# Stick-breaking attention with its later sums on top of the scores, values of two pairs in split passes, and a new order of the mixed phase

## What is computed

```python
def stick_breaking_attention(h, w_in, w_out):
    q, k, v = jnp.split(h @ w_in, 3, axis=-1)          # 16 heads of 64
    ...
        z = jnp.einsum('bhqd,bhkd->bhqk', qb, k) * scale
        past = k_pos[None, :] < q_pos[:, None]
        log_beta = jax.nn.log_sigmoid(z)
        log_keep = jnp.where(past, jax.nn.log_sigmoid(-z), 0.0)
        later = lax.cumsum(log_keep, axis=3, reverse=True) - log_keep
        a = jnp.where(past, jnp.exp(log_beta + later), 0.0)
        return jnp.einsum('bhqk,bhkd->bhqd', a, v)
    ...
    return merge_heads(o) @ w_out
```

## Time and profile before

| | |
|---|---|
| median of 3 runs | 2287.86 us (2287.84 to 2290.86) |
| profiled execution | 2294.6 us, span 2292.8 us |
| PE busy | 2175.9 us, 95% |
| DVE busy | 1593.8 us, 70% |
| ACT busy | 1094.7 us, 48% |
| mean granted TensorE clock | 0.982 |

### The profile page before, as it was taken

One profiled execution on the slowest core, in us unless ns is written; L12 is line 12 of the kernel. 1 busy time (PEld: TensorE's weight loads), 2 busy tenths in 40 slices (PEclk: granted clock), 3 DMA queues, 4 the chain that ended last, 5 costly groups with the idle time before them and its releaser, 6 DMA issues.

```text
span 2292.8 us, 44979 instructions
## 1 busy us (share of the span) xinstructions
PE 2175.9 (95%) x17598; PEld 2068.1 (90%) x17598; DVE 1593.8 (70%) x2647; ACT 1094.7 (48%) x1755; POOL 0.2 (0%) x4
## 2 busy tenths in 40 slices
PE   7889999998899999998999999999898999998999
PEld 6788899987888999897999887999787999897999
DVE  6585688865857888666787766788777855666544
ACT  4454444445445444555444455444465444555443
POOL 0000000000000000000000000000000000000000
PEclk9999999999999999999999999999999999999999
DMA  5454499845445998443799644799544875442664
GB/s 159 130 142 139 144 299 299 282 127 137 131 129 165 300 304 274 132 134 104 259 301 301 182 130 129 231 302 299 165 113 137 285 202 174 129 137 83 188 187 147
DMA packets 546483, 436.40 MB, mean 190 GB/s; under 512 B 27680, under 2 KB 472264, under 8 KB 546248
## 3 DMA queue, kind: packets, MB, share of 16 engines
q1 hardware_dynamic: 545208, 433.16, 62.1%
q10 hardware_dynamic: 1168, 1.77, 0.2%
HBM read 433.82 MB, written 1.05 MB: 190 GB/s over the span
## 4 chain that ended last, share of the span: by engine, by line
PE 83%; DVE 8%; ACT 4%; DVEq 1%; issue 1%; DMA 1%; SPq 1%; ACTq 0%
PE bank L690 13%; PE bank L692 13%; PE bank L691 13%; PE acc L690 8%; PE acc L692 7%; PE acc L691 7%; PE bank L840 3%; PE bank L898 2%; PE bank L1214 2%; PE bank L700 2%; DVE w_lo L1840 1%; ACT w_hi L1349 1%; PE bank L761 1%; PE bank L762 1%; PE bank L765 1%
## 5 line engine op out<-in xcount | busy, mean ns | idle before, releaser
L1349 ACT ACTIVATE w_hi<-wslot 128x1024 fp32r<-128x1024 f32 x590 | 611.5, 1055 | 532.8 <-PE acc L692 250.6
L690 PE MATMUL bank<-h_hi,w_hi 128*128 128x256 f32 x2784 | 792.6, 285 | 21.7 <-DVE w_lo L1831 7.8
L691 PE MATMUL bank<-h_lo,w_hi 128*128 128x256 f32 x2784 | 778.0, 279 | 0.0
L692 PE MATMUL bank<-h_hi,w_lo 128*128 128x256 f32 x2784 | 777.8, 279 | 0.0
L1840 DVE TENSOR_TENSOR w_lo<-wslot,w_hi 128x1024 fp32r<-128x1024 f32 x412 | 493.7, 1221 | 214.9 <-ACT w_hi L1349 214.2
L690 PEld LDWEIGHTS bank<-h_hi,w_hi 128*128 128x128 f32 x2784 | 526.3, 189 | 39.7 <-DVE w_lo L1831 13.6
L691 PEld LDWEIGHTS bank<-h_lo,w_hi 128*128 128x128 f32 x2784 | 531.0, 191 | 2.3 <-issue 1.7
L692 PEld LDWEIGHTS bank<-h_hi,w_lo 128*128 128x128 f32 x2784 | 526.0, 189 | 0.0
L690 PE MATMUL acc<-mid_hi,w_hi 128*128 128x256 f32 x1120 | 318.0, 284 | 6.3 <-DVE mid_lo L2180 3.2
L692 PE MATMUL acc<-mid_hi,w_lo 128*128 128x256 f32 x1120 | 313.0, 279 | 0.0
L691 PE MATMUL acc<-mid_lo,w_hi 128*128 128x256 f32 x1120 | 313.0, 279 | 0.0
(11 more groups left out here) (288 smaller groups left out, 2970.7 us busy)
## 6 DMA issues: line engine op xcount, KB each, us to landing
wslot<-in_ada_w_dram SPq DMA_DIRECT2D x192, 512.0 KB, 5.8
wslot<-in_ffn_w_gate_dram SPq DMA_DIRECT2D x88, 512.0 KB, 4.9
wslot<-in_ffn_w_up_dram SPq DMA_DIRECT2D x88, 512.0 KB, 5.5
wslot<-in_ffn_w_down_dram SPq DMA_DIRECT2D x88, 512.0 KB, 3.7
wslot<-in_w_in_dram SPq DMA_DIRECT2D x72, 512.0 KB, 5.1
wslot<-in_sb_w_in_dram SPq DMA_DIRECT2D x48, 512.0 KB, 4.9
wslot<-in_w_ffn_gate_dram SPq DMA_DIRECT2D x44, 512.0 KB, 4.7
wslot<-in_w_ffn_up_dram SPq DMA_DIRECT2D x44, 512.0 KB, 5.3
```

Source lines behind the costliest of these rows:

```text
L690: pe.matmul(dst, w_hi[:, w, cols], hi, start=start, stop=False, skip_group_check=True)
L691: pe.matmul(dst, w_hi[:, w, cols], lo, start=False, stop=False, skip_group_check=True)
L692: return pe.matmul(dst, w_lo[:, w, cols], hi, start=False, stop=stop, skip_group_check=True)
L1349: return act.activation(dst, src, ACT.Copy)
```

## The change

It has three parts.

**Stick-breaking.** Scores and later sums are now one accumulation in PSUM: the scores don't end their group, the later sums go on top with masked negative log terms in `lb`, and `end_weights` subtracts `sm` from the bank. The scale of the scores moves into ACT's copy of the query. ACT reads the scores straight from PSUM. The values of two pairs are projected at once in three split passes from slots 2 and 4 (`V_SLOTS`), so each has a `w_hi` and `w_lo` of its own (`PART_V`), and `hT` isn't made for these layers. The order on all engines is new: after the scores of pair j come the output of pair j-1, the query of j+1, the later sums of j, the key of j+1, the values of j, half of the values' projection of the next two pairs, and the scores of j+1.

**Mixed phase.** Some operations trade places on PE, ACT and DVE. **Sliding window.** Unit 2's parts are made inside pair 0.

```diff
 # schedule: norm no longer makes hT for "sb"
-        if split != "ffn" or more["stack"] == 1:
+        if split == "ffn" and more["stack"] == 1 or split == "att" and more["att"] != "sb":
             counts.update(h_ready=KT)
...
 # SP, stick-breaking (need = uses of the slot that must be over)
+                        query_and_key([offs[c] + P for c in range(2)], [u[c] + 2 for c in range(2)])
+                        out_rows(0, u[3] + 1)
                         first_units(2, l, u[SLOT_FF:SLOT_FF + 2])
+                        values([offs[2] + 2 * P + b * P for b in range(2)], [u[V_SLOTS[b]] + 2 for b in range(2)])
+                        query_and_key([offs[c] + 2 * P for c in range(2)], [u[c] + 3 for c in range(2)])
...
 # PE, stick
                 def scores(i, first=False):
                     pe.wait_ge(sem["qk_ready"], g("qk_ready") + i + 1)
+                    if not first:
+                        pe.wait_ge(sem["y_ready"], g("y_ready") + i)
...
-                        pe.matmul(bank[:, 2 + hh, 0:256], C("later"), sm[:, hh, 0:256], start=True, stop=False)
+                        pe.matmul(bank[:, 2 + hh, 0:256], C("later"), lb[:, hh, 0:256], start=False, stop=False, skip_group_check=True)
...
-                        mm = pe.matmul(B(1, 256 + P * t, 384 + P * t), hT[:, k, P * t:P * t + P], wk(2, k),
-                                       start=(k == 0), stop=(k == KT - 1))
+                        high, low = (w[:, PART_V:PART_V + 2, k_cols(k)] for w in (w_hi, w_lo))
+                        pe.matmul(dst, h_hi[:, k, tokens], high, start=(k == 0), stop=False, skip_group_check=True)
+                        pe.matmul(dst, h_hi[:, k, tokens], low, start=False, stop=False, skip_group_check=True)
+                        mm = pe.matmul(dst, h_lo[:, k, tokens], high, start=False, stop=(k == KT - 1), skip_group_check=True)
...
+                def whole(m, b, first=False, more=True, v=True):
+                    j = 2 * m + b
+                    if not first:
+                        out(j - 1)
+                    if more:
+                        query(j + 1)
+                    later_sums(j)
+                    if more:
+                        key(j + 1)
+                    values(m, b)
+                    if v:
+                        project_v(m + 1, b)
+                    if more:
+                        scores(j + 1)
...
 # ACT, stick
+                    softplus(j)
+                    if b == 0:
+                        v_high(m + 1)
+                    act.wait_ge(unit_done[3], g("unit_done3") + j)
+                    out_high(j)
+                    exps(j)
+                    act.wait_ge(unit_done[0], g("unit_done0") + j + 2)
+                    mix_high(0, 0, unit_loads(at, "sb", 0, j + 2))
+                    qk_copy(j + 1)
+                    y_high(j)
+                    mix_high(1, 1, unit_loads(at, "sb", 1, j + 2))
+                    if b == 1:
+                        v_copy(m + 1)
...
 # DVE, stick
+                        dve.wait_ge(sem["sb_log"], g("sb_log") + 2 * i + hh + 1)
+                        stt(sm[:, hh, :], z, 0.0, pr[:, hh, :], ALU.max, ALU.add)
+                        dve.drain()
+                        stt(lb[:, hh, :], sm[:, hh, :], -1.0, C("past")).then_inc(sem["sb_spm"], 1)
...
+                    softplus(j)
+                    if b == 0:
+                        v_low(m + 1)
+                    else:
+                        mix_low(3, PART_DOWN, j)
+                    end_weights(j)
+                    if b == 0:
+                        mix_low(3, PART_DOWN, j)
+                    mix_low(0, 0, j + 2)
+                    out_low(j)
+                    mix_low(1, 1, j + 2)
...
+                softplus(n - 1)
+                mix_low(3, PART_DOWN, n - 1)
+                low(0, 2, g("w_high") + 3)
+                end_weights(n - 1)
+                out_low(n - 1)
...
 # PE, mixed phase: ssd_tokens is cut in two, ssd_products is its second half
+                def ssd_products(gr):
                     after("ssd_cumc", gr + 1)
...
                 out(12, 0, mix_y[0])
+                ssd_products(1)
                 out(13, 1, mix_y[0])
...
                 gla_scores(1)
+                after("gla_yl", 1)
+                out(28, 0, mix_y[0], hi=4)
                 gla_values(1)
-                after("gla_yl", 1)
-                out(28, 0, mix_y[0])
+                out(28, 0, mix_y[0], lo=4)
...
 # ACT, mixed phase
-                gate_exps(0)
...
+                unit_high(11)
                 ssd_square(0)
-                unit_high(11)
                 ssd_root(0)
                 unit_high(12)
                 unit_high(13)
+                ssd_silu(1)
                 y_high("ssd", 0, mix_y[0])
-                ssd_silu(1)
...
+                gate_exps(0)
                 ssd_square(1)
...
 # DVE, mixed phase
                 unit_low(3)
+                unit_low(4)
                 convolve(0, 0)
-                unit_low(4)
-                gate(0)
                 unit_low(5)
...
                 unit_low(9)
+                unit_low(10)
+                unit_low(11)
                 ssd_gated(0)
-                unit_low(10)
                 convolve(1, 0)
-                unit_low(11)
                 convolve(1, 1)
+                ssd_normed(0)
                 unit_low(12)
-                ssd_normed(0)
+                y_low("ssd", 0, mix_y[0])
                 unit_low(13)
-                y_low("ssd", 0, mix_y[0])
...
                 unit_low(16)
+                gate(0)
                 ssd_gated(1)
...
 # ACT and DVE, sliding window (here ACT; DVE with qk_low and next_low alike)
-                if att == "swa":
-                    qk_high(2)
...
-                    if att != "swa":
+                    if att != "swa" or i == 0:
                         next_high(i + 2)
```

More of the change, by code:

```diff
@@ L121 @@
 PART_SECOND = 3
+PART_V = 2
+V_SLOTS = (2, 4)
 def split_index(what, f):
@@ new lines, in stick @@
+                v_high(0)
+                qk_copy(0)
+                for c in range(2):
+                    mix_high(c, c, unit_loads(at, "sb", c, 1))
+                v_copy(0)
+                with act.Fori(0, n // 2 - 1) as m:
+                    whole(m, 0)
+                    whole(m, 1)
+                softplus(n - 2)
+                act.wait_ge(unit_done[3], g("unit_done3") + n - 2)
+                out_high(n - 2)
+                exps(n - 2)
+                act.wait_ge(unit_done[0], g("unit_done0") + n)
@@ L1897, in stick, with v_low @@
[L1897 to L1901 removed]
+                def v_low(m):
+                    for b in range(2):
+                        dve.wait_ge(sem["v_high"], g("v_high") + 2 * m + (b + 1))
+                        part = PART_V + b
+                        dve.tensor_tensor(w_lo[:, part, :], wslot[:, V_SLOTS[b], :], w_hi[:, part, :], ALU.subtract)\
+                           .then_inc(slot_used[V_SLOTS[b]], 1)
```

237 lines of the change are left out of this document (118 added, 119 removed).

## The result

The median fell from 2287.86 us to 2259.68 us (3 runs, 2254.85 to 2259.87). The ratio is 0.9861 (95% interval 0.984 to 0.9881), so 31.8 us are gained, 27 to 37 by the interval. The forecast was 18.6 (2269.3, range 2258 to 2279).

The account below looks back on a forecast made before the run. TensorE (PE), busy 95% of the span, was taken as the bound, so only its work or waits could pay. Stick-breaking -16.8, mixed phase -6.6 and sliding window +4.8 sum to -18.6 us: 2269.3 from 2287.9, range 2258 to 2279.

Parts of the forecast that it names:

- the mixed phase: Two mixed layers: reordering cuts PE's waits by 2.3 and 1.0 us a layer, -6.6 us in all.
- the edges of SB: Start and end of each stick-breaking layer: start waits lose 1.4 us, clock returns 0.8, the end gains 1.5.
- Values in three passes, and the loop: Stick-breaking loop: three split passes save 0.94 us a pair, 7.5 a layer; pairs take 14.80 us without waits.
- the clock at both ends: Stick-breaking layer: lower-clock loss recovered, 0.8 us at the start and 1.6 at the last later sums.
- the 1.3 that I expected at `ssd_state(1)` and `unit_low(15)`: Mixed layer in the new order: PE still waits 1.3 us at these two operations.
- the 0.5 ahead of the squares: Mixed layer: moving half of out(28) covers a 1.5 us wait but leaves 0.5 us more before the squares.
- the first wait: Mixed layer: PE's longest wait for w_lo, 2.0 us, goes by putting unit_low(4) before convolve(0, 0).
- The waits for `w_lo` (1.75) and `y_ready` (1.1): Stick-breaking edges: PE waits about 1.75 us for w_lo at the start, 1.1 for y_ready before pair 7's scores.
- S+5.6: Stick-breaking loop: the second head is ready 5.6 us after the scores start, 1.0 us early for the later sums.
- the loss that I took back by half: Start of a stick-breaking layer: 1.6 us lost to the lower clock behind the waits, 0.8 of it recovered.
- SWA (+4.8): Sliding-window start: the output rows' load, queued behind unit 2's late w_lo, goes out 4.8 us later, costing +4.8.
- Rival one: Sliding window costs nothing, load not held or earlier maxima repay it: -23 to -26 us, 2262 to 2264; chance 0.13.

Follow-up runs that it names:

- e15: Changed kernel with the third split pass (h_lo times high weights) left out of the stick-breaking values' projection; 2239.3 us, one execution.
- e8: Kernel before with one mixed-phase edit, unit_low(4) ahead of convolve(0, 0) on DVE; 2293.2 us, one execution.
- e10: Kernel before with unit_low(4) ahead of convolve(0, 0), and gate(0) with gate_exps(0) at their late places; 2293.4 us, one execution.
- e5: Changed kernel with the first output rows loaded ahead of unit 3 in SWA's pair 0 only; median 2257.0 us, ratio 0.9852.
- e6: Changed kernel with SWA's output rows loaded ahead of unit 3 in all pairs, and unit 3's high half behind pair 0's pt copies; 2254.8 us, ratio 0.984.
- e2: Kernel before with the mixed phase's new order alone; median 2277.6 us, ratio 0.9924.
- e11: Kernel before with half of out(28) ahead of gla_values(1) in the mixed phase, nothing else; 2289.4 us, one execution.

## Why the prediction was off

The step that failed is the size of two terms, the mixed phase most and the edges of SB next. Stage by stage, in profiled executions (means are those of the table above):

1. **Values in three passes, and the loop (-7.5 a layer): right.** 14.74 for 14.80; e15 bears out the price of a pass (0.90 for 0.94). PE's busy time in a layer fell by 9.7, forecast 9.9 (7.5 and 2.4 for the clock at both ends).
2. **Mixed phase (-3.3 a layer, -6.6): the term that was mis-sized most.** It came to -15.3 between the two profiles, -17 by the means. No clock was in the term, with no reason given, though SB's term had one: by the means PE's busy time fell by 8.5 us in the two layers for the same work, as their mean granted clock rose from 0.95 to 0.97 and from 0.97 to 0.99. The idle time fell by 8.8, since the 1.3 that I expected at `ssd_state(1)` and `unit_low(15)` and the 0.5 ahead of the squares did not come. The reason given for the first wait was wrong as well (`unit_low(4)` alone only moves it, e8; it goes when `gate(0)` leaves too, e10). Which of the moves frees the clock is open.
3. **Edges of SB (waits, +1.4 at the start and 7.7 to 7.8 at the end): mis-sized.** The waits for `w_lo` (1.75) and `y_ready` (1.1) came as said, 1.71 and 1.04. The others were shorter: later sums 0.4 for 1.15 and for 0.9, values 0.5 for 1.4 and 3.3 for 4.1, the last output 1.0 for 1.7; in all 3.7 a layer. The traces tell why. From the end weights to the last `pt` it takes 2.17 us at both edges, not the 2.6 that I took from a middle pair, where the second head's weights wait for PE. At the end of the layer a `w_lo` of 1.22 us on DVE held up `y_lo` before; now it stands ahead of the end weights. The softplus chain was sized right (second head ready 5.42 us after the start of the scores for S+5.6); there the wait is shorter because PE comes later than said, and because a row counts PE idle only from the end of the last product's record, which is 0.28 us long where the next step comes after 0.11. So a wait worked out by steps can't be set against a row as it stands. Counted by the starts of products, which has no such fault, an SB layer goes as follows (means of the 18 layers without and the 12 with the part; the forecast's terms put to the same stretches):

   | stretch of an SB layer | without | with | | forecast |
   |---|---|---|---|---|
   | to pair 1's scores | 32.0 | 29.8 | -2.2 | -1.4 |
   | to pair 7's scores | 94.3 | 86.6 | -7.6 | -7.3 |
   | to the last output product | 13.2 | 12.4 | -0.8 | +0.4 |
   | behind it | 8.5 | 8.4 | -0.1 | 0 |

   So the end missed by 1.2 (0.5 of it because the stretch before takes 13.2 us, where I had added up 12.7), the start by 0.8. At the start 8 of the 18 layers without the part ran a stretch at the lower level (32.7 us for 31.4 in the others), none of the 12 with it: the loss that I took back by half went whole. By the means the two layers missed the forecast by 4.7.
4. **SWA (+4.8): right in size**, +4.1 by the means, +6 to +8 by medians. The mechanism was half right: the late load is what ACT waits for, but unit 3's load is in series with it (e5), and PE's wait for unit 2's own `w_lo` is as large a part of the price (3.0; 2.5 in e6). The Trainium skill, DMA: Bandwidth & Descriptors, on which this rested, says that a DMA's semaphore wait is over on the issuing sequencer before dispatch (in its section "Anatomy of one DMA — SWDGE (gpsimd) path", not the one that the prediction names). The trace agrees: the `w_lo` ended at 1633.77, unit 3's load was issued at 1633.79 and the output rows' behind it, at 1634.20.
5. **Last block: not in the forecast**, -6.2 in the profiles, cause open.

The sum with these, between the two profiled executions: -18.6 - 7.3 - 8.7 + 1.7 - 6.2 = -39.1 of 39.7. In the profiled execution of before both SB layers were at the long end of the table's extremes, so the means are the fairer size there. Between the totals (-31.8 for -18.6) the mixed phase's miss, some 10 us by the means and by the ratio of e2, is most of the 13. Rival one (no cost in SWA, -23 to -26) is the nearest in size, which is luck: SWA did cost what was forecast.

## What to carry to other kernels

A stage's difference should be split into PE's busy and idle time before it is explained: in the mixed phase the busy half (the clock) was as large as the waits. An idle time worked out from steps and one read from a row are not the same measure; compare starts with starts. Before an operation is moved to end a wait, look at what else stands ahead of the next operand on that engine: the wait may only move to it. A load that is moved behind a late `w_lo` holds back what is in series with it as well as what is queued behind it, so the repair of the queue alone gives back a part only.

## What the hardware showed that was not expected

A removed wait of 1.46 us (e11, one execution) went with 6.2 us in one layer and 0.4 in its twin: the granted clock of that stretch went from 0.72 to 1.00 in the first, and the second layer's mean fell from 0.98 to 0.96.

Unbroken streams of the same 256-column products at a granted clock of 1.00 have two rates, one step every 113 or every 118 ns, in every profiled execution of either kernel. A stream keeps its rate until something interrupts it (1620 of 1652 streams), and in one without an interruption, as in the last block, the 4% between them become 6 us. The Trainium skill, TensorE: Matmul & The Clock Gate ("Wait — 56ns, not 53.3ns?"), gives one rate (N / 2.4 GHz plus about 2.5 ns, by estimate 109 ns at 256 columns); the traces show 113 and 118, and the measurement decides.
